# Limited differences of decays on ScalarE's rectifier, and a group's scaling placed beside the last heads, in a two-block decoder kernel

## The chip, the cores and the metric

The kernel runs on one core of a Trainium2 chip. The metric is the device time of one execution in microseconds, the lower the better. Everything is float32 or float32r in memory of the chip; the weights come from HBM.

## What is computed

The input x has 512 positions of 1024 features. The reference is a block of two layers (a state-space mixer and a convolved feed-forward; differential attention and another convolved feed-forward) and a second block (three mixed branches, cross attention, a gated feed-forward). The change touches the state-space mixer alone, whose core is:

```python
def segsum(a):
    cs = jnp.cumsum(a, axis=-1)
    d = cs[..., :, None] - cs[..., None, :]
    return jnp.where(mask, d, -jnp.inf)      # lower triangle

decay_in = jnp.exp(segsum(ac))                                   # per head and chunk, 128 x 128
cb = jnp.einsum('bclgn,bcsgn->bcgls', cc, bc)
y_diag = jnp.einsum('bcgls,bgrcls,bcsgrp->bclgrp', cb, decay_in, xc)
y_off = jnp.einsum('bclgn,bcgrpn,bgrcl->bclgrp', cc, states_in, jnp.exp(a_cs))
...
y = y + xs32 * d_skip.astype(jnp.float32)[:, None]
y = y.reshape(b, s, D_INNER) * jax.nn.silu(z.astype(jnp.float32))
y = rms_norm(y.reshape(b, s, SSM_GROUPS, D_INNER // SSM_GROUPS), ...).reshape(b, s, D_INNER)
return y @ out_w
```

There are 32 heads of 64 features in four groups of eight, and four chunks of 128 positions. Since the decays are sums of negative numbers, a difference cs[l] - cs[s] with l at or behind s is never above 0; in the other triangle it is limited to 0 before the exponential, so that nothing overflows, and the product with the masked cb takes it out.

## The kernel before, in words

**Data.** Activations lie with features on partitions and the 512 positions along the row: one tile of 128x512 for each 128 features. A matrix product is made in float32r from two halves of each operand, a rounded one ("hi", made by ScalarE) and the rest ("lo", made by VectorE), with three matmuls for each 128x128 block of weights. Weights are streamed: SyncE loads units of up to 128x1024 into three buffers, ScalarE rounds them (line 1536 for most), VectorE takes the rest (a cut, line 1972).

**Order of the work.** A planner (class Plan) writes the order down before anything is built. Its time is a tick: one piece of a weight product on TensorE, six matmuls of 128x512, after the small work that is due at that tick. `once(name, key, test, windows)` starts a piece of work at the first tick at which its test holds and PSUM banks are free for its windows. Each engine's program then walks over the ticks, and in a tick over its own list of duties in the order in which they stand in the source; `at("pair", T - 2)` means the duty of every pair that was started two ticks ago. Each engine issues in this order, and waits on semaphores where data comes from another engine (`full` and `empty` of a PSUM bank, and named signals such as `sub`, `edec`, `yadd`).

**State-space stage.** Per group g: six tiles of the convolved inputs (`in`), four gate tiles (`z`), statistics of the chunk states (`sta`, `stb`), then four pairs of heads, three ticks apart, then `gate` (product with the gate tiles, squares, their sums), `rms`, `yn` (scaling by the norm and the splitting in hi and lo as operand Y of the output product), and `out` (eight tiles of the output product, two ticks each). In the plan before, pairs (3,0) to (3,3) start at ticks 179, 182, 185 and 188, the scaling of group 2 at tick 192, gate 3 at 196, rms 3 at 204; `out 1` runs over ticks 181 to 196, `out 2` over 197 to 212, `out 3` from 213. The first group's pairs start at ticks 48, 51, 54 and 57, the second's at 73 to 82, the third's at 123 to 132, the scaling of group 1 at 125.

**A pair (g, p), started at tick t**, with two heads k:

- t, TensorE: two matmuls 64*128 64x512 spread the row of cumulated decays over all partitions, into banks `s0` and `s1`.
- t+1, VectorE (lines 2183 to 2195): for each head and chunk, `ts(d, bank, css, SUB, 0.0, MIN)`: row minus the column of the partition, limited to 0, 128x128 each, eight operations; they wait for the row, and for TensorE's `by` of the pair before the last, which read the same buffer.
- t+2, ScalarE (lines 1673 to 1684): for each head an exponential of the spread row itself (64x384, out of the bank, into `ep`), which waits for the differences of that head and for GpSimd's `yadd` of the pair before the last, and empties the bank; then for each head the exponential of the whole difference tile, 128x512.
- t+3, TensorE: `bo`, the product with the states. GpSimd (line 2546): the two difference tiles times the masked cb (128x512 each).
- t+4, VectorE: `bo` times `ep` (128x384).
- t+5, TensorE: `by`, matmuls 128*64 128x128 for both heads and all chunks.
- t+6, VectorE: the skip term; t+7, GpSimd: the sum (128x384).

Beside this run, on ScalarE, the first tap and the tanh of each convolution, the tanh of each gate tile, the squares of `gate`, the hi halves of Y, and at the end of a tick the rounding of a weight unit. In ScalarE's list a tanh of a convolution comes ahead of the pair's exponentials. VectorE has for each convolution three taps and a product (line 1975), for `yn` four products at ticks T to T+3 and four rests at T+2 to T+5, for `gate` four products in one tick, ahead in the list of `yn` and behind the pair's duties; the cut of a weight unit is last in a tick. Helpers record most operations, so line 1972 is any two-tile operation of VectorE, 1975 any scalar-tensor-tensor, 1980 a tensor-scalar with two operations, 1536 a ScalarE copy, 1539 a ScalarE function, 2546 a two-tile operation of GpSimd, 1142 a matmul.

The condition that places the scaling of groups 2 and 3 is in `free` in the planner (line 409):

```python
return ("z", 3, 3) in self.end and (g == 3 or self.past("pair", (3, 3), 4))
```

Of the kernel before, what the change touches and what calls it, by code (L numbers as in the profile page):

```python
# [13 lines left out]
ACT = mybir.ActivationFunctionType  # L14
MUL, ADD, SUB, MIN, MAX, POW = ALU.mult, ALU.add, ALU.subtract, ALU.min, ALU.max, ALU.pow
AX = mybir.AxisListType.X

P = 128
# [3 lines left out]
NT = S // P  # L22
# [131 lines left out]
class Plan:  # L154
# [22 lines left out]
    def at(self, name, t):  # L177
        return self.starts.get(name, {}).get(t, ())
# [182 lines left out]
    def ssm(self):  # L361
# [24 lines left out]
        def have(keys, more=0):  # L386
            return all(k in silu and self.T >= silu[k] + more for k in keys)

        for g in range(4):
            self.once("sta", g, lambda g=g: have([("in", g, 0), ("in", g, 1)], 4)  # L390
                      and (g == 0 or self.past("pair", (g - 1, 3), 6)), [(("bt", g), 0, 2), (("scb", g), 0, 2)])
            self.once("stb", g, lambda g=g: have([("in", g, i) for i in range(2, 6)], 2) and self.past("sta", g, 2)
                      and self.past("dec", 0, 13),
                      [(("xc", g, c), c, 2) for c in range(NT)] + [(("st", g, c), 5 + 2 * c, 2) for c in range(3)])
            for p in range(4):
                self.once("pair", (g, p), lambda g=g, p=p: self.past("stb", g, 8)
                          and (p == 0 or self.past("pair", (g, p - 1), 3)),
                          [(("s0", g, p), 0, 3), (("s1", g, p), 0, 3), (("bo", g, p), 3, 2), (("by", g, p), 5, 2)])
            self.once("gate", g, lambda g=g: self.past("pair", (g, 3), 8) and have([("z", g, i) for i in range(4)], 1))

            def squares(g=g):
                if self.when("gate", g) == self.T:
                    for i in range(1, 4):
                        self.sq_n[("g", g), i] = len(self.sq_n)
                if self.past("gate", g, 8 if g in (0, 3) else 11) and self.when("rms", ("g", g)) is None:
                    self.rms(("g", g))

            self.rules.append(squares)

            def free(g=g):  # L410
                if g == 0:
                    return self.past("tabs", 0, 48)
                if g == 1:
                    return ("out", 0, 7) in self.end
                return ("z", 3, 3) in self.end and (g == 3 or self.past("pair", (3, 3), 4))

            self.once("yn", g, lambda g=g, free=free: self.past("rms", ("g", g), 6) and free())

            def parts(g=g):
                if self.when("yn", g) == self.T:  # L420
                    for i in range(4):
                        self.lo[f"Y{g}", i] = self.T + 2 + i

            self.rules.append(parts)
# [531 lines left out]
def by_block(ap, n=32):  # L956
    return ap.rearrange("p (j h) -> p j h", h=n)


def again(ap, n):  # L960
    return ap.unsqueeze(1).to_broadcast([P, n, ap.shape[1]])
# [18 lines left out]
class Kernel:  # L980
# [12 lines left out]
    def full(self, key):  # L993
        return self.sig.bank[self.plan.bank[key]].full, self.turn(key)
# [7 lines left out]
    def leave(self, key):  # L1002
        return self.sig.bank[self.plan.bank[key]].empty, 1
# [525 lines left out]
def scalar_program(eng, K):  # L1529
    plan, buf, sig, dram = K.plan, K.buf, K.sig, K.dram  # L1530
    at, full, empty, leave = plan.at, K.full, K.empty, K.leave
    w = Waits(eng)
    pc = buf.pc

    def copy(out, in_, scale=1.0):
        return eng.activation(out, in_, ACT.Copy, scale=scale)  # L1536

    def func(f, out, in_, bias=0.0, scale=1.0, accum=None):
        return eng.activation(out, in_, f, bias=bias, scale=scale, accum_out=accum)  # L1539
# [78 lines left out]
    def ssm(T):  # L1618
        for key in at("conv", T - 1):
            _, g, i = key  # L1620
# [10 lines left out]
        for key in at("conv", T - 3):  # L1631
            _, g, i = key
# [3 lines left out]
        for key in at("zsilu", T - 1):  # L1636
            _, g, i = key
# [30 lines left out]
        for g in at("stb", T - 6):  # L1668
            w.wait_ge(*full(("st", g, 0)))
            if g:  # L1670
                w.wait_ge(*full(("bo", g - 1, 3)))
            copy(buf.St[:, 0, :], K.of(("st", g, 0))[:, :]).then_inc(*leave(("st", g, 0)))
        for g, p in at("pair", T - 2):
            n = 4 * g + p
            e_ = buf.ep[n % 2]
            for k in range(2):
                rows = slice(64 * k, 64 * k + 64)
                w.wait_ge(*sig["sub"].at(g, p, k))
                if n >= 2:
                    w.wait_ge(*sig["yadd"].at((n - 2) // 4, (n - 2) % 4))  # L1680
                func(ACT.Exp, e_[rows, P:S], K.of((f"s{k}", g, p))[rows, P:S]).then_inc(*leave((f"s{k}", g, p)))
            for k in range(2):
                d = buf.hd[2 * (n % 2) + k]
                func(ACT.Exp, d[:, :], d[:, :]).then_inc(*sig["edec"].up(g, p, k))
        for age, ii in ((1, (0, 1)), (2, (2,)), (3, (3,))):
            for g in at("gate", T - age):
                for i in ii:
# [277 lines left out]
def vector_program(eng, K):  # L1965
    plan, buf, sig = K.plan, K.buf, K.sig
    at, full, empty, leave = plan.at, K.full, K.empty, K.leave
    w = Waits(eng)
    pc = buf.pc

    def tt(out, a, b, o):
        return eng.tensor_tensor(out, a, b, o)  # L1972
# [4 lines left out]
    def ts(out, a, s0, o0, s1=None, o1=None):  # L1977
        if o1 is None:
            return eng.tensor_scalar(out, a, s0, None, o0)  # L1979
        return eng.tensor_scalar(out, a, s0, s1, o0, o1)  # L1980
# [138 lines left out]
    def ssm(T):  # L2119
        for _ in at("dec", T - 2):  # L2120
            bank = K.of(("d1",))
# [15 lines left out]
        for _ in at("dec", T - 8):  # L2137
            bank = K.of(("d2",))
# [3 lines left out]
            for j in range(NT):  # L2142
                t = eng.tensor_copy(by_block(buf.csd[:, j, :]), again(buf.css[:, 32 * j:32 * j + 32], 4))
            t.then_inc(*sig["csd"].up())
            tt(buf.tail[:, :], bank[:, P:2 * P], buf.css[:, :], SUB).then_inc(*sig["tail"].up())
        for _ in at("dec", T - 13):
            w.wait_ge(*sig["csh"].at())
            for rows in LOW_ROWS:
                t = tt(buf.csT[rows, :], K.of(("d3",))[rows, :], buf.csT[rows, :].bitcast(F), SUB)
# [27 lines left out]
        for g, p in at("pair", T - 4):  # L2177
# [2 lines left out]
            w.wait_ge(*empty(("s0", g, p)))  # L2180
            w.wait_ge(*empty(("s1", g, p)))
            tt(e_[:, P:S], K.of(("bo", g, p))[:, P:S], e_[:, P:S], MUL).then_inc(*leave(("bo", g, p)))
        for g, p in at("pair", T - 1):
            n = 4 * g + p
            for k in range(2):
                d, bank = buf.hd[2 * (n % 2) + k], K.of((f"s{k}", g, p))
                w.wait_ge(*full((f"s{k}", g, p)))
                w.wait_ge(*sig["cs"].at())
                if n >= 2:
                    w.wait_ge(*full(("by", (n - 2) // 4, (n - 2) % 4)))  # L2190
                for c in range(NT):
                    a = slice(c * P, c * P + P)
                    col = 32 * c + 8 * g + 2 * p + k
                    t = ts(d[:, a], bank[:, a], buf.css[:, col:col + 1], SUB, 0.0, MIN)
                t.then_inc(*sig["sub"].up(g, p, k))
        for g, p in at("pair", T - 6):
            xs = buf.XS[g % 2][:, p, :]
            w.wait_ge(*full(("by", g, p)))
# [17 lines left out]
        for key in at("conv", T - 2):  # L2216
            _, g, i = key
# [6 lines left out]
        for key in at("conv", T - 4):  # L2224
            _, g, i = key
# [3 lines left out]
        for key in at("zsilu", T - 2):  # L2229
            z = buf.ZT[key[1] % 2][:, key[2], :]  # L2230
# [601 lines left out]
```

## Time and profile before

| | |
|---|---|
| median of three runs | 2459.2 us (2458.94 to 2461.61) |
| the profiled execution | 2459.41 us, its span in the trace 2457.6 us |
| mean granted TensorE clock | 0.995 |
| TensorE busy | 2418.4 us, 98% |
| VectorE busy | 1398.4 us, 57% |
| ScalarE busy | 972.2 us, 40% |
| GpSimd busy | 406.3 us, 17% |

The state-space stage fills about the first 430 us of the span. In the profile, times are microseconds from the span's start, PE is TensorE's matrix unit, DVE VectorE, ACT ScalarE and POOL GpSimd. The granted clock is the share of full speed (2.4 GHz) that the throttle gave TensorE. Ends of matmuls are modelled, so an idle time of PE is a little smaller than the distance that it makes in the starts.

### The profile page before, as it was taken

What the parts mean: (1) busy time and instruction counts of PE and PEld (TensorE: products, weight loads), DVE (VectorE), ACT (ScalarE), POOL (GpSimd) and SP (SyncE); (2) the same over time, 40 slices, a digit from 0 to 9 for tenths busy, and PEclk for the clock granted to TensorE, in tenths of its full rate; (3) what the DMA queues carried; (4) which work ended last, traced back from release to release, by engine and by line L of the source; (5) the groups of instructions that cost most, each with busy time, mean ns of one, the idle gap of its engine ahead of it and who ended that gap; (6) DMA issues with size and microseconds to landing.
All of it is one profiled execution on the core that took longest, in us unless ns stands there. A gap on an engine that the chain in (4) does not pass through costs nothing.

```text
span 2457.6 us, 30359 instructions
## 1 busy us (share of the span) xinstructions
PE 2418.4 (98%) x11930; PEld 1963.1 (80%) x11930; DVE 1398.4 (57%) x2286; ACT 972.2 (40%) x1595; POOL 406.3 (17%) x320
## 2 busy tenths in 40 slices
PE   8899999999999999999999999999999999999998
PEld 6677777888888887878888887787788887888887
DVE  6878876663665445576546547534565445343342
ACT  5444434442344444454334434424443334322223
POOL 0352332220111222122002100001220101110011
PEclk9999999999999999999999999999999999999999
DMA  4532222223223221132232242231234322223222
GB/s 160 101 88 86 78 69 77 95 94 102 96 84 122 65 69 51 48 113 97 90 105 91 81 137 78 69 112 53 65 120 134 120 87 85 98 91 102 96 84 87
DMA packets 74269, 226.23 MB, mean 92 GB/s; under 512 B 8080, under 2 KB 12304, under 8 KB 74000
## 3 DMA queue, kind: packets, MB, share of 16 engines
q1 hardware_dynamic: 69696, 215.90, 27.2%
q10 hardware_dynamic: 4432, 8.39, 2.0%
q8 instruction: 95, 1.56, 0.3%
q14 instruction: 46, 0.38, 0.0%
HBM read 215.87 MB, written 8.39 MB: 91 GB/s over the span
## 4 chain that ended last, share of the span: by engine, by line
PE 59%; issue 0%; DVE 0%; ACT 0%; POOL 0%; POOLq 0%; DVEq 0%
PE bank L1142 58%; PE bank L1146 1%; ACT t L1536 0%; DVE t L1972 0%; DVE t L1979 0%; DVE t L1975 0%; ACT t L1539 0%; POOL t L2546 0%; POOLq L2767 0%; DVEq L2767 0%; DVE t L2468 0%; DVE t L2474 0%; POOLq L765 0%
## 5 line engine op out<-in xcount | busy, mean ns | idle before, releaser
L1142 PE MATMUL bank<-t 128*128 128x512 f32 (+4 forms) x11412 | 2388.0, 375 | 29.2 <-DVE t L1972 14.9
L1142 PEld LDWEIGHTS bank<-t 128*128 128x128 f32 (+1 forms) x11412 | 1907.7, 186 | 468.2 <-issue 85.3
L1536 ACT ACTIVATE t<-t 128x1024 fp32r<-128x1024 f32 (+5 forms) x649 | 549.3, 856 | 684.2 <-PE bank L1142 277.3
L1972 DVE TENSOR_TENSOR t<-t 128x1024 fp32r<-128x1024 f32 (+6 forms) x686 | 624.7, 921 | 251.4 <-ACT t L1536 246.4
L2546 POOL TENSOR_TENSOR t<-t 128x512 f32<-128x512 f32 (+5 forms) x240 | 365.7, 1530 | 1650.6 <-ACT t L1539 549.0
L1972 DVE TENSOR_TENSOR t<-bank,t 128x512 f32<-128x512 f32 (+4 forms) x410 | 275.6, 676 | 490.1 <-PE bank L1142 472.3
L1539 ACT ACTIVATE t<-t 128x512 f32<-128x512 f32 (+5 forms) x545 | 330.6, 616 | 536.9 <-DVE t L1972 328.1
L1975 DVE SCALAR_TENSOR_TENSOR t<-t 128x512 f32<-128x512 f32 (+6 forms) x430 | 321.1, 752 | 94.8 <-ACT t L1539 54.0
L1536 ACT ACTIVATE t<-bank 128x512 f32<-128x512 f32 (+4 forms) x150 | 71.5, 493 | 130.5 <-PE bank L1146 90.6
L2549 POOL TENSOR_SCALAR t<-t 128x128 f32<-128x128 f32 (+3 forms) x64 | 40.0, 630 | 389.0 <-ACT t L1536 252.7
L1146 PE MATMUL bank<-t 128*128 128x128 f32 x518 | 81.5, 275 | 2.1 <-ACT t L1536 1.0
L1975 DVE SCALAR_TENSOR_TENSOR t<-t,bank 128x512 f32<-128x512 f32 x64 | 46.1, 721 | 63.2 <-PE bank L1142 49.5
L1146 PEld LDWEIGHTS bank<-t 128*128 128x128 f32 x518 | 62.9, 141 | 18.1 <-DVE t L1983 3.0
L1983 DVE CUSTOM_DVE_ANT_0 t<-bank,t 128x256 f32<-128x256 f32 (+3 forms) x128 | 55.6, 463 | 18.9 <-PE bank L1142 16.3
L1975 DVE SCALAR_TENSOR_TENSOR t<-bank,t 128x512 f32<-128x512 f32 x32 | 22.1, 690 | 60.3 <-PE bank L1142 60.3
L1539 ACT ACTIVATE t<-bank 64x384 f32<-64x384 f32 (+2 forms) x41 | 20.5, 501 | 50.2 <-DVE t L1980 28.6
L1979 DVE TENSOR_SCALAR t<-t 128x256 f32<-128x256 f32 (+6 forms) x88 | 33.7, 384 | 2.9
L1980 DVE TENSOR_SCALAR t<-bank,t 128x128 f32<-128x128 f32 x128 | 34.4, 340 | 0.5 <-PE bank L1142 0.5
L1536 ACT ACTIVATE t<-bank,t 128x256 f32<-128x256 f32 (+2 forms) x40 | 16.9, 482 | 39.1 <-PE bank L1142 37.4
L1980 DVE TENSOR_SCALAR t<-bank 128x4 f32<-128x4 f32 (+2 forms) x37 | 6.0, 161 | 35.1 <-PE bank L1142 35.0
L1539 ACT ACTIVATION_READ_ACCUMULATOR t<-t 128x1 f32 x128 | 24.2, 189 | 0.0
L1539 ACT ACTIVATE t<-bank,t 128x256 f32<-128x256 f32 x16 | 7.6, 474 | 37.7 <-DVE t L2468 37.7
(26 smaller groups left out, 60.1 us busy)
## 6 DMA issues: line engine op xcount, KB each, us to landing
t<-in_w SPq DMA_DIRECT2D x304, 512.0 KB, 3.4
t<-in_w SPq DMA_DIRECT2D x48, 384.0 KB, 3.0
t<-in_w SPq DMA_DIRECT2D x56, 320.0 KB, 2.9
t<-in_w SPq DMA_DIRECT2D x28, 256.0 KB, 3.2
tab<-t ACTq DMA_DIRECT2D x1, 2560.0 KB
t<-in_x SPq DMA_DIRECT2D x8, 256.0 KB, 5.6
t<-tab SPq DMA_DIRECT2D x8, 256.0 KB, 3.8
spill<-t ACTq DMA_DIRECT2D x1, 2048.0 KB, 8.2
```

The lines of the kernel that those rows point to most:

```text
L1142: return eng.matmul(out, lhs, rhs, start=start, stop=stop, skip_group_check=loose)
L1146: return eng.transpose(out, in_, ident[0:n, 0:n])
L1536: return eng.activation(out, in_, ACT.Copy, scale=scale)
L1539: return eng.activation(out, in_, f, bias=bias, scale=scale, accum_out=accum)
L1972: return eng.tensor_tensor(out, a, b, o)
L1975: return eng.scalar_tensor_tensor(out=out, in0=a, scalar=s, in1=b, op0=o0, op1=o1)
L1979: return eng.tensor_scalar(out, a, s0, None, o0)
L1980: return eng.tensor_scalar(out, a, s0, s1, o0, o1)
L1983: return eng.tensor_tensor_reduce(out, a, b, 1.0, FMAX, ADD, MIN, m)
L2546: return eng.tensor_tensor(out, a, b, o)
L2549: return eng.tensor_scalar(out, a, s, s1, o, o1)
```

## The change

The limited differences of a pair leave VectorE's list and stand in ScalarE's, one tick after the pair's start as before. ScalarE computes them with the opposite sign: Relu(-row + column), the column being the bias of each partition and -1.0 the scale. The exponential that follows has the scale -1.0, which turns the sign back. The exponentials of the spread row no longer wait for the differences of their head but for the row alone (they follow the differences in ScalarE's own order), and the exponentials of the difference tiles now have the wait for them. In the planner, the scaling of group 2 waits for pair (3, 2) plus 3 ticks in place of pair (3, 3) plus 4.

```diff
@@ class Plan, ssm, free
-                return ("z", 3, 3) in self.end and (g == 3 or self.past("pair", (3, 3), 4))
+                return ("z", 3, 3) in self.end and (g == 3 or self.past("pair", (3, 2), 3))
@@ scalar_program, ssm
+        for g, p in at("pair", T - 1):
+            n = 4 * g + p
+            for k in range(2):
+                d, bank = buf.hd[2 * (n % 2) + k], K.of((f"s{k}", g, p))
+                w.wait_ge(*full((f"s{k}", g, p)))
+                w.wait_ge(*sig["cs"].at())
+                if n >= 2:
+                    w.wait_ge(*full(("by", (n - 2) // 4, (n - 2) % 4)))
+                for c in range(NT):
+                    a = slice(c * P, c * P + P)
+                    col = 32 * c + 8 * g + 2 * p + k
+                    t = func(ACT.Relu, d[:, a], bank[:, a], buf.css[:, col:col + 1], -1.0)
+                t.then_inc(*sig["sub"].up(g, p, k))
         for g, p in at("pair", T - 2):
             n = 4 * g + p
             e_ = buf.ep[n % 2]
             for k in range(2):
                 rows = slice(64 * k, 64 * k + 64)
-                w.wait_ge(*sig["sub"].at(g, p, k))
+                w.wait_ge(*full((f"s{k}", g, p)))
                 if n >= 2:
                     w.wait_ge(*sig["yadd"].at((n - 2) // 4, (n - 2) % 4))
                 func(ACT.Exp, e_[rows, P:S], K.of((f"s{k}", g, p))[rows, P:S]).then_inc(*leave((f"s{k}", g, p)))
             for k in range(2):
                 d = buf.hd[2 * (n % 2) + k]
-                func(ACT.Exp, d[:, :], d[:, :]).then_inc(*sig["edec"].up(g, p, k))
+                w.wait_ge(*sig["sub"].at(g, p, k))
+                func(ACT.Exp, d[:, :], d[:, :], scale=-1.0).then_inc(*sig["edec"].up(g, p, k))
@@ vector_program, ssm
-        for g, p in at("pair", T - 1):
-            n = 4 * g + p
-            for k in range(2):
-                d, bank = buf.hd[2 * (n % 2) + k], K.of((f"s{k}", g, p))
-                w.wait_ge(*full((f"s{k}", g, p)))
-                w.wait_ge(*sig["cs"].at())
-                if n >= 2:
-                    w.wait_ge(*full(("by", (n - 2) // 4, (n - 2) % 4)))
-                for c in range(NT):
-                    a = slice(c * P, c * P + P)
-                    col = 32 * c + 8 * g + 2 * p + k
-                    t = ts(d[:, a], bank[:, a], buf.css[:, col:col + 1], SUB, 0.0, MIN)
-                t.then_inc(*sig["sub"].up(g, p, k))
```

## Rows read from the trace of the kernel before

**Rows 1.** Page, part 1: busy time, share of the span and instructions of each engine

```profile
PE 2418.4 (98%) x11930; PEld 1963.1 (80%) x11930; DVE 1398.4 (57%) x2286; ACT 972.2 (40%) x1595; POOL 406.3 (17%) x320
```

**Rows 2.** Waits of TensorE, 0 to 460 us: total us, times, longest

```profile
PE bank L1142 <- DVE t L1972: 13.2, 9, 3.0
...
PE bank L1142 <- ACT t L1539: 2.4, 1, 2.4
```

**Rows 3.** TensorE's timeline, 345 to 455 us: start, length, tiles, count, idle time before

```profile
369.94 0.96 PE L1142 MATMUL bank<-t 128*128 128x512 f32 x3 [0.69 <-DVE t L1972]
372.96 1.65 PE L1142 MATMUL bank<-t 128*128 128x512 f32 x3 [2.05 <-DVE t L1972]
375.77 15.93 PE L1142 MATMUL bank<-t 128*128 128x512 f32 x65 [1.16 <-DVE t L1972]
...
401.95 36.21 PE L1142 MATMUL bank<-t 128*128 128x512 f32 x155 [1.97 <-DVE t L1972]
```

**Rows 4.** TensorE's timeline, 103 to 118 us

```profile
104.04 9.35 PE L1142 MATMUL bank<-t 128*64 128x128 f32 x64 [0.85 <-DVE t L1972]
115.80 2.58 PE L1142 MATMUL bank<-t 64*128 64x512 f32 x8 [2.41 <-ACT t L1539]
```

**Rows 5.** TensorE's timeline, 246 to 256 us

```profile
255.23 0.98 PE L1142 MATMUL bank<-t 128*64 128x128 f32 x14 [1.25 <-POOL t L2546]
```

**Rows 6.** TensorE in four stretches: length, busy (matmuls), granted clock, DMA share, GB/s

```profile
368.90:379.60 10.70, 6.79 (x17) 0.68 0.15 49
500.00:550.00 50.00, 50.00 (x223) 1.00 0.27 87
113.20:120.20 7.00, 4.58 (x14) 0.76 0.61 105
249.75:252.20 2.45, 2.45 (x14) 1.00 0.00 0
```

**Rows 7.** VectorE's timeline, 360 to 376 us (a merged row may hold several tile types)

```profile
366.52 1.51 DVE L1972 TENSOR_TENSOR t<-t 128x512 fp32r<-128x512 f32 x1
...
369.21 4.83 DVE L1972 TENSOR_TENSOR t<-t 128x512 fp32r<-128x512 f32 x7
...
374.56 1.16 DVE L1972 TENSOR_TENSOR t<-t 128x512 fp32r<-128x512 f32 x1
```

**Rows 8.** Groups by form, 93 to 375 us: count, busy us, mean ns, idle before

```profile
L1980 DVE TENSOR_SCALAR t<-bank,t 128x128 f32<-128x128 f32 x128 | 34.4, 340 | 0.5 <-PE bank L1142 0.5
...
L1539 ACT ACTIVATE t<-bank 64x384 f32<-64x384 f32 x32 | 15.5, 485 | 37.5 <-DVE t L1980 28.6 <-POOL t L2546 8.7
```

**Rows 9.** Busy time of PE, PEld, DVE, ACT, POOL; then clock, DMA share, GB/s

```profile
94.00:129.00 35.00, 31.66 (x180) 23.52 (x180) 29.44 (x58) 16.45 (x27) 17.74 (x12) 0.95 0.60 109
```

**Rows 10.** Groups of ScalarE by form, 0 to 420 us

```profile
L1539 ACT ACTIVATE t<-bank 128x128 f32<-128x128 f32 x1 | 0.3, 258 | 0.0
```

**Rows 11.** ScalarE's timeline, 405 to 408 us: copy with a column as scale, square without

```profile
405.71 0.72 ACT L1536 ACTIVATE t<-t 128x512 fp32r<-128x512 f32 x1 [2.80 <-DVE t L1972]
406.34 0.62 ACT L1539 ACTIVATE t<-t 128x512 f32<-128x512 f32 x1
```

**Rows 12.** ScalarE's timeline, 102 to 118 us

```profile
108.75 1.06 ACT L1536 ACTIVATE t<-t 128x1024 fp32r<-128x1024 f32 x1
114.61 0.63 ACT L1539 ACTIVATE t<-t 128x512 f32<-128x512 f32 x1 [4.80 <-DVE t L1975]
...
115.27 0.99 ACT L1539 ACTIVATE t<-bank 64x384 f32<-64x384 f32 x2
116.28 1.67 ACT L1539 ACTIVATE t<-t 128x512 f32<-128x512 f32 x3
```

**Rows 13.** VectorE's timeline, 102 to 118 us

```profile
110.20 2.15 DVE L1980 TENSOR_SCALAR t<-bank,t 128x128 f32<-128x128 f32 x8
112.27 2.31 DVE L1975 SCALAR_TENSOR_TENSOR t<-t 128x512 f32<-128x512 f32 x3
```

**Rows 14.** GpSimd's timeline, 244 to 262 us

```profile
249.69 6.34 POOL L2546 TENSOR_TENSOR t<-t 128x512 f32<-128x512 f32 x3 [4.34 <-ACT t L1539]
257.86 4.48 POOL L2546 TENSOR_TENSOR t<-t 128x512 f32<-128x512 f32 x3 [1.82 <-ACT t L1539]
```

## The prediction

> **What bounds the kernel now.** I read the page first: TensorE is busy for 98% of the span [rows 1]. So an edit on another engine is worth only what it takes out of TensorE's stops, and the next view is the list of TensorE's waits over the first 460 us, which hold the state-space stage [rows 2]. It is short: 13.2 us on VectorE's line 1972 in nine stops, and 2.4 us on ScalarE in one. Then each stop is found in TensorE's timeline. Three lie in a row where the third group's output projection begins: 0.69, 2.05 and 1.16 us [rows 3]. One of 2.41 us lies at the fourth pair of the first group, with 0.85 us before it [rows 4]. One of 1.25 us lies in the third group [rows 5].
>
> A stop costs more than its idle time, since the clock falls behind it. Undisturbed, 223 matmuls start in 50 us, one each 0.225 us [rows 6]. Around the three stops 17 start in 10.70 us, at a mean granted clock of 0.68: at full pace they take 17 x 0.225 = 3.8, so this place costs **6.9 us**. Around the 2.41 us stop 14 matmuls take 7.00 us; the same 14 (two row spreads of 64x512, six of 128 columns, six of 512) take 2.45 us in the third group, so this place costs **4.55 us** [rows 6].
>
> **What holds the three stops.** Time in this kernel's program is a tick, one weight piece on TensorE. Walking the planner's rules, pair (3,3) starts at tick 188, group 2's scaling (yn) at 192, gate 3 at 196, and out 2's first matmul is at tick 197. Each engine issues in tick order. VectorE writes the second halves of Y2 at ticks 194 to 197, so the last two stand behind the four gate products of tick 196: one merged row of seven operations, 4.83 us long, from 369.21 [rows 7]. TensorE's starts at 369.94, 372.96 and 375.77 each follow such a write. The last one, 1.16 us from 374.56, ends 0.05 us before the third start.
>
> **The change, part by part.**
> *yn 2 four ticks earlier.* The new rule, pair (3,2) plus 3, is met at tick 188; its other conditions (statistics from 155, z 3 finished at 180) are met long before. The twelve vector operations (four scalings on VectorE, four roundings on ScalarE, four rests on VectorE) keep their number and move to ticks 188 to 193, all ahead of the gate and four ticks ahead of out 2. At 6 x 0.225 = 1.35 us a tick the cover is over 5 us, against 1.5 us for the dearest rest [rows 7]. No DMA moves; the weight cut of tick 192 now stands behind fewer operations. **Term A: -6.9 us** (0 if something else is as late; -6.9 is all there is). The 1.97 us stop at group 3's projection [rows 3] hangs on statistics taken 8 ticks after gate 3, whose tick does not change: 0.
>
> *The limited differences leave VectorE.* 128 operations, 34.4 us in all, 0.269 each, so 2.15 per pair [rows 8]. VectorE is busy 29.44 of 35.00 us around the first group's pairs; ScalarE 16.45 [rows 9].
>
> *They come to ScalarE.* The trace has no Relu. The nearest row is a ScalarE operation on a 128x128 bank tile, 258 ns [rows 10]; one with a column as scale takes 0.72 against 0.62 us without [rows 11], so +0.1 for the pointer. Three operations of 128x512 span 1.67 us [rows 12] where alone each takes 0.62, so neighbours overlap by some 0.1. Hence 0.26 us apart and **2.2 us per pair**, the same as on VectorE. Bounds: 0.16 apart if the pointer is free (1.4 per pair), and 0.62 apart if a short tile costs what 512 columns do (5 us). I take 0.26, the nearest row.
>
> The Trainium skill (ScalarE: Activation LUTs, Rules for kernel authors) speaks against this: relu belongs on VectorE. The row agrees on no such loss, 0.26 against 0.27 us for this fp32 tile out of a bank. The same page (What ACT_TABLE_LOAD costs) gives 186 ns + 0.833 per column + 93 per pointer with 93 overlap, an estimate of 0.29 us apart and 2.35 per pair; the sum would be the same within its bounds.
>
> What covers it: ScalarE now stands idle for 28.6 us in front of its bank exponentials, waiting for just these differences [rows 8]. VectorE starts them late because in its order a product that needs the previous pair's second matmul comes first. On ScalarE they start when the row spread lands. The chain from there is: differences 2.2, two bank exponentials 1.0, the first exponential of a whole tile 0.6, GpSimd's two products. It grows by 0.5 to 1, since the bank exponentials no longer overlap the differences. With 16 pairs and the mean wait of 28.6 / 16 = 1.8 us given back, most pairs gain about 1 us of slack; the first pair of each group, where VectorE was prompt, loses about 1.
>
> *Group 0.* The chain of the 2.41 us stop reads backwards as: row spread of pair (0,3) waits for the bank that the exponential at 115.27 empties; this stands behind a tanh at 114.61, which idled 4.80 us for the taps on VectorE; the taps (112.27, 2.31 us) stand behind eight differences (110.20, 2.15) [rows 12, 13]. By then VectorE has issued 24 of these, 6.4 us. With them gone the taps are done near 110. ScalarE's own queue is next: weight split at 108.75, eight Relus to 112.0, tanh to 112.6, exponential to 113.1, against TensorE ready at 113.2 for the spread. So a remainder of about 0.3: **Term B: -4.2** (0 to -4.55).
>
> *Pair (0,0).* Its 0.85 us stop is on VectorE's bank product; that comes 2 us earlier, but the exponentials follow the eight Relus, and GpSimd's products end near 104 too. **Term C: -0.3** (-0.85 to +0.9).
> *Pair (2,1).* TensorE waits 1.25 us for GpSimd, whose three operations take 6.34 us where the next pair's take 4.48 [rows 5, 14]: group 1's scalings run on VectorE beside them. They start some 0.5 us earlier. **Term D: -0.4** (-1.25 to +1). Term A puts yn 2 beside pair (3,3) in the same way; a like stretch of 2 us there falls into the slack that the earlier exponentials give: 0.
> *Pair (1,0).* Relus behind a tanh and before a split and a square move the first product of GpSimd from 154.3 to about 155.9, so the state matmul may wait: **Term E: +0.5** (0 to +1.6).
>
> Sum: -6.9 - 4.2 - 0.3 - 0.4 + 0.5 = **-11.3**. The profiled execution took 2459.41, 0.2 above the median of 2459.2 shown, so it goes to 2448.1 and the median to about **2448**. Everything behind 450 us is the same program.
>
> **Rivals.** 0.2% is 4.9 us, about what a measurement of this kernel can tell from no change.
> 1. *Forecast*, 2448: chance 0.58.
> 2. *Only A comes.* ScalarE has 27 operations in 35 us around group 0 [rows 9] and gets 32 more with the four pairs, 8.8 us: 25 of 35 us busy, with waits in order (and little room within a pair, rival 4). If the tanh or the split (its weights arrive just at 108.7) holds the Relus, the stop at the fourth pair comes back under ScalarE's name: 2459.2 - 6.9 = 2452. For it: the thin margin in B. Against it: VectorE's 6.4 us. 0.25.
> 3. *Only B comes.* The roundings of Y2 stand behind pair (3,3)'s Relus and exponentials on ScalarE, and out 2 still waits: 2459.2 - 4.4 = 2455, within 0.2%. Against it: four ticks. 0.05.
> 4. *Slower: ScalarE becomes the bound of the pairs.* Place: every pair. A pair comes each 6.2 us at full pace (two ticks 2.7, the 14 matmuls 2.45, the state matmuls 1.0 [rows 5, 6]). ScalarE has 2.1 us of exponentials in it (0.99, and two of the three in 1.67 [rows 12]), the rest of its 16.45 us over some 14 ticks, 1.7 per three, and now 2.2: 6.0. The margin is thin, though only four pairs come in a row and the groups beside output projections hold fewer taps. At the bound of 5 us for eight Relus it loses 2.6 x 16 = 42, and the total is 2459 - 7 + 42, near 2494. It decides against the change from 0.7 us lost per pair, 3.1 us for eight Relus, 0.39 apart. 0.06. A change of ScalarE's function table at each Relu would act alike; the trace shows tanh, exponential and copy beside each other without one. The Trainium skill (ScalarE: Activation LUTs, Table sets: the hidden batching unit) says relu is in every set, which no run here shows yet.
> 5. *Nothing*: both stops are replaced by equals, 2459. 0.06.
>
> **How the numbers follow.** Faster by over 0.2%: rivals 1 and 2 and a little of 3, 0.84; within: 3 and 5, 0.09; slower: 4 and a little of 5, 0.07. Range: all the gains at their ends, 2459.2 - 6.9 - 4.55 - 0.85 - 1.25 = 2445.6, taken as 2445; rival 2 with E and C at their dear ends, 2452.3 + 2.5, 2454.8, taken as 2454.5.
>
> **What would show it.** In the profile after: no stop of TensorE on line 1972 at out 2, and granted clock 1.0 there; the stop at the fourth pair of group 0 gone or under 0.5 us; ScalarE busy 35 us more, VectorE 34 less; 128 ScalarE operations of 128x128 at about 0.35 us, 0.26 apart; no new table load; ScalarE's idle time before the bank exponentials mostly gone. Wrong would be: Relus over 0.39 us apart, a new stop at each state matmul on GpSimd, or lateness of Y2 under ScalarE's name.

## The result, and the profile after

| | before | after |
|---|---|---|
| median (lowest to highest), four runs each | 2459.07 us (2458.46 to 2461.61) | 2444.97 us (2442.07 to 2446.79) |
| ratio to before | | 0.9943, 95% interval 0.993 to 0.9955 |
| the profiled execution, its span | 2459.41, 2457.6 us | 2445.11, 2443.3 us |
| mean granted clock | 0.995 | 0.997 |

The kernel is 14.1 us faster by the medians of four runs each (11 to 17 by the interval), where 11 had been forecast. The first part of the page of the kernel after answers to [rows 1]:

```profile
PE 2412.1 (99%) x11930; PEld 1959.0 (80%) x11930; DVE 1367.6 (56%) x2158; ACT 1004.5 (41%) x1723; POOL 403.0 (16%) x320
```

VectorE has 128 instructions and 30.8 us less, ScalarE 128 and 32.3 us more. TensorE does the same 11930 matmuls in 6.3 us less of busy time: a matmul at half clock counts as busy for twice as long, so what stood behind the stops went with them. The waits of TensorE over 0 to 460 us answer to [rows 2]:

```profile
PE bank L1142 <- DVE t L1986: 8.5, 5, 3.0
...
PE bank L1142 <- ACT t L1539: 0.8, 2, 0.5
```

Line 1986 of the kernel after is line 1972 of before (VectorE's two-tile operations), 1989 is 1975, and 2547 is GpSimd's 2546. VectorE's share fell from 13.2 us in nine stops to 8.5 in five, ScalarE's from one of 2.4 to two with 0.8. Of the five, the two longest, 3.0 us each, are ahead of all the pairs and are in every kernel of this case. TensorE's timeline of the kernel after shows where the rest is, against [rows 3 to 5]:

```profile
86.81 25.09 PE L1142 MATMUL bank<-t 128*128 128x512 f32 x128 [2.98 <-DVE t L1986]
112.43 13.29 PE L1142 MATMUL bank<-t 64*128 64x512 f32 x82 [0.53 <-ACT t L1539]
...
245.53 16.66 PE L1142 MATMUL bank<-t 64*128 64x512 f32 x101 [0.30 <-ACT t L1539]
...
349.62 29.26 PE L1142 MATMUL bank<-t 128*128 128x512 f32 x156
...
389.14 31.13 PE L1142 MATMUL bank<-t 128*128 128x512 f32 x133 [1.97 <-DVE t L1986]
```

The row from 86.81 runs without a stop past 102.55, where the state matmuls of pair (0,0) now start: the 0.85 us is gone. The 2.41 us stop is 0.53. The 1.25 us stop on GpSimd is gone, and 0.30 us stands at the row spread of the pair behind it. The row from 349.62 holds the beginning of out 2 with no stop at all. The stop of 1.97 us at out 3 is there as before, 12.81 us sooner. Around out 2's start (the same columns as [rows 6], then those of [rows 9]) TensorE keeps its clock:

```profile
366.00:377.00 11.00, 11.00 (x54) 9.22 (x53) 5.71 (x9) 2.13 (x2) 4.53 (x3) 1.00 0.44 143
```

54 matmuls in 11.00 us at a clock of 1.00, where 17 stood in 10.70 us at 0.68 [rows 6]. The groups by form of the kernel after, 93 to 375 us, answer to [rows 8]:

```profile
L1539 ACT ACTIVATE t<-bank,t 128x128 f32<-128x128 f32 x128 | 34.7, 382 | 8.4 <-PE bank L1142 8.2
...
L1539 ACT ACTIVATE t<-bank 64x384 f32<-64x384 f32 x32 | 15.6, 487 | 2.4 <-POOL t L2547 2.0
```

A Relu lasts 382 ns by itself, and 34.7 / 128 = 0.27 us passes from one to the next, 2.17 us per pair. The tensor-scalar it replaces lasted 340 ns, with 34.4 / 128 = 0.27 between two [rows 8]. ScalarE's idle time in front of the bank exponentials fell from 37.5 to 2.4 us; 8.4 us now stand in front of the Relus, nearly all of it for TensorE's row spread. No table load was added: three up to 420 us, in both traces.

**Where the 14.3 us of the profiles lie.** The starts of the same matmuls in the two traces:

| start of | before | after | shift | new since the row above |
|---|---|---|---|---|
| row spread of pair (0,0) | 93.32 | 92.90 | -0.42 | start of the program |
| state matmuls (`by`) of (0,0) | 104.04 | 102.55 | -1.49 | -1.07, term C |
| `by` of (0,3) | 127.98 | 123.04 | -4.94 | -3.45, term B |
| `by` of (1,0) | 158.92 | 154.23 | -4.69 | +0.25, term E |
| `by` of (2,3) | 267.94 | 262.34 | -5.60 | -0.91, term D |
| `by` of (3,3) | 361.82 | 356.22 | -5.60 | 0 |
| out 3, behind its stop | 401.95 | 389.14 | -12.81 | -7.21, term A |
| end of the span | 2457.6 | 2443.3 | -14.3 | -1.5, none |

The last row has no cause in the change. Near 970 us in the trace after, and near 980 in that before, in the attention, both traces have the same stop of 1.67 us on VectorE; the clock falls behind it in one trace and not in the other. The windows around it, of the kernel before and then of the kernel after:

```profile
980.00:990.00 10.00, 10.00 (x72) 9.50 (x70) 4.71 (x18) 4.34 (x14) 1.57 (x2) 0.83 0.18 59
```

```profile
965.00:975.00 10.00, 8.33 (x69) 7.68 (x69) 6.84 (x25) 5.39 (x17) 2.16 (x3) 1.00 0.18 59
```

A mean of 0.83 over 10 us is 3.4 us at half speed, 1.7 us lost, about what the last row of the table shows. It does not follow the edits: of the twelve kernels' profiles in this case, the clock falls there in those of before, e7, e9, e10 and e11, and not in the other seven. The first row is not the change's either, since the first pair starts anywhere from 92.14 to 95.02 us in these profiles. So some 12.4 us of these two traces are the change's, and 1.9 are chance of this pair of executions.

### The profile page after: what moved, and what is told of

Same layout as the page of the kernel before. It is cut to its first block, busy times and chain, and to the rows that moved or that the text cites. A ratio compares the mean times of both kernels' runs of the same rounds, so it can differ in the third digit from the quotient of the medians.

```text
span 2443.3 us, 30351 instructions
## 1 busy us (share of the span) xinstructions
PE 2412.1 (99%) x11930; PEld 1959.0 (80%) x11930; DVE 1367.6 (56%) x2158; ACT 1004.5 (41%) x1723; POOL 403.0 (16%) x320
## 4 chain that ended last, share of the span: by engine, by line
PE 59%; issue 0%; DVE 0%; ACT 0%; POOL 0%; POOLq 0%; DVEq 0%
PE bank L1142 58%; PE bank L1146 1%; ACT t L1536 0%; DVE t L1986 0%; DVE t L1993 0%; DVE t L1989 0%; ACT t L1539 0%; POOL t L2547 0%; POOLq L2768 0%; DVEq L2768 0%; DVE t L2469 0%; DVE t L2475 0%; POOLq L765 0%
## 5 line engine op out<-in xcount | busy, mean ns | idle before, releaser
L1539 ACT ACTIVATE t<-bank,t 128x128 f32<-128x128 f32 (+1 forms) x144 | 42.3, 392 | 46.1 <-DVE t L2469 37.7
L1539 ACT ACTIVATE t<-bank 64x384 f32<-64x384 f32 (+2 forms) x41 | 20.6, 503 | 15.2 <-PE bank L1142 12.8
```

## The experiments

Each was timed beside runs of the kernel before on the same chip. The ratio is to those; their medians were 2458.52 (e1 to e4), 2457.76 (e5, e7, e9, e11) and 2458.87 us (e6, e10).

### Each part alone: e1_only_yn and e2_only_relu

e1 is the kernel before with this edit alone:

```diff
-                return ("z", 3, 3) in self.end and (g == 3 or self.past("pair", (3, 3), 4))
+                return ("z", 3, 3) in self.end and (g == 3 or self.past("pair", (3, 2), 3))
```

> Group 2's scaling at tick 188, the limited differences still on VectorE. Theory (the three stops at out 2 come from the order of ticks alone): they go, the stops at the first group's pairs (0.85 and 2.41 us) and the 1.25 us one stay, time about 2459.1 - 7.2 = 2452, within 1.5. Rival (the two parts need each other: with the differences still in its list VectorE does the earlier scalings late, or makes a state matmul of group 3 wait): a new stop of over 1 us between 340 and 370 us, time 2454 to 2459.

Measured: 2452.82 us (2449.52 to 2456.56, 11 runs), ratio 0.9977, interval 0.9968 to 0.9986. TensorE's timeline of e1:

```profile
104.61 9.35 PE L1142 MATMUL bank<-t 128*64 128x128 f32 x64 [0.84 <-DVE t L1972]
116.35 4.19 PE L1142 MATMUL bank<-t 64*128 64x512 f32 x14 [2.40 <-ACT t L1539]
...
362.76 23.03 PE L1142 MATMUL bank<-t 128*64 128x128 f32 x114 [0.32 <-POOL t L2546]
...
396.04 4.18 PE L1142 MATMUL bank<-t 128*128 128x512 f32 x17 [1.97 <-DVE t L1972]
```

The three stops of out 2 are gone and the first group's stand, so this edit acts at that place alone. Its pair (0,0) starts 0.56 us later than in the trace of before; less that, out 3 comes 5.91 + 0.56 = 6.5 us sooner. A new 0.32 us on GpSimd stands at the state matmuls of (3,3): there the scaling's operations run on VectorE beside GpSimd's products. The theory's 2452 came (2452.82), and the rival's stop of over 1 us did not.

e2 is the kernel after with the old rule, `(3, 3), 4`.

> The limited differences on ScalarE, group 2's scaling at tick 192 as before. Theory (each part clears its own stops): the first group's and the 1.25 us stop go as in the changed kernel, 5.6 us up to the last pair; at out 2 the stops at the third and fourth operand stay, since the four gate products still come first, though VectorE reaches them a little earlier: 4 to 7 us lost there, time about 2453. Rival (lateness of VectorE, and not the order, made out 2 wait): the three stops go too, time 2446.

Measured: 2449.24 us (2445.7 to 2451.32, 5 runs), ratio 0.9961, interval 0.9948 to 0.9973. TensorE's timeline of e2:

```profile
365.31 0.98 PE L1142 MATMUL bank<-t 128*128 128x512 f32 x3 [0.98 <-DVE t L1986]
368.12 15.76 PE L1142 MATMUL bank<-t 128*128 128x512 f32 x65 [1.83 <-DVE t L1986]
...
394.13 6.25 PE L1142 MATMUL bank<-t 128*128 128x512 f32 x26 [1.97 <-DVE t L1986]
```

The first group is as in the kernel after, but at out 2 two stops are left of three, 2.81 us of idle time instead of 3.90. VectorE, rid of the differences, is less late there also without the new place of the scaling. So the parts overlap: counted from the first pair's start to out 3, they bring 6.5 and 7.4 us alone (the latter 401.95 - 394.13, less 0.46 of an earlier start), 13.9 together if they were independent, and 12.4 in fact. I had expected about 2453 for e2 and missed by nearly 4 us. The place was as the theory said, two stops left at the third and fourth operand, and out 3 comes 5.0 us later than in the kernel after. But I had not counted the 2.2 us that VectorE's relief gives there, and e2's profile gains another 3.1 us behind out 3, where the clock fell neither at the stop of 1.97 us nor near 970 us. e2 also holds the changed waits of the exponentials; what they are worth without moving the differences was not tried.

### ScalarE's margin: e4_relu_twice

The kernel after, with each Relu done a second time into a tile that nobody reads:

```diff
+                    spare = ...
+                    func(ACT.Relu, spare, bank[:, a], buf.css[:, col:col + 1], -1.0)
                     t = func(ACT.Relu, d[:, a], bank[:, a], buf.css[:, col:col + 1], -1.0)
```

> Each limited difference is computed twice on ScalarE, the first time into a spare tile: 2.2 us more per pair. It measures how much room ScalarE has in a pair. Theory (a pair comes each 6.2 to 6.6 us and ScalarE fills 6.0 of it where convolutions run): groups 0 and 1 lose 1.5 to 2 us per pair, groups 2 and 3 less, in all 12 to 25 us, time 2457 to 2470. Rival (ScalarE's idle time elsewhere absorbs it): under 4 us, time below 2449.

Measured: 2459.48 us (2457.84 to 2461.41, 10 runs), ratio 1.0004, interval 0.9995 to 1.0013, and 14.5 above the kernel after. Groups by form of ScalarE, 93 to 375 us, then TensorE's timeline, of e4:

```profile
L1539 ACT ACTIVATE t<-bank,t 128x128 f32<-128x128 f32 x256 | 67.7, 415 | 6.3 <-PE bank L1142 6.0
...
L1539 ACT ACTIVATE t<-bank 64x384 f32<-64x384 f32 x32 | 16.1, 503 | 0.4
```

```profile
107.70 6.72 PE L1142 MATMUL bank<-t 64*128 64x512 f32 x42 [1.63 <-ACT t L1539]
115.61 14.86 PE L1142 MATMUL bank<-t 64*128 64x512 f32 x82 [1.19 <-ACT t L1539]
```

This is the slower rival made real: once ScalarE has 2.1 us more per pair (67.7 less 34.7, over 16), it is never idle before a bank exponential (0.4 us in all), and TensorE waits for it at the row spreads, whose bank it empties. 33 us of work cost 14.5, so some 18.5 were still free, 1.2 us per pair. The time lies in the theory's range; the loss per pair was smaller than it said, 8.3 us against the kernel after by the end of the second group, 1.0 per pair where 1.5 to 2 had been expected. Since e4 takes what before takes, it is about the break-even itself: 67.7 / 16 = 4.2 us of Relus per pair, where the prediction had put it at 3.1.

### Less on ScalarE: e3_head_each

The kernel after, with head 0 of each pair on ScalarE and head 1 on VectorE as before (its exponential keeps the scale 1.0):

```diff
@@ scalar_program
-            for k in range(2):
+            for k in range(1):
...
                     t = func(ACT.Relu, d[:, a], bank[:, a], buf.css[:, col:col + 1], -1.0)
@@ vector_program
+            for k in range(1, 2):
...
+                    t = ts(d[:, a], bank[:, a], buf.css[:, col:col + 1], SUB, 0.0, MIN)
```

> Head 0 of each pair on ScalarE, head 1 on VectorE, four operations each. Theory (the 0.53 and 0.30 us stops left are ScalarE's queue being full by a little): ScalarE is relieved by 1.1 us per pair, both go, time 2443 to 2445. Rival (VectorE's queue in group 0 was the real bound, with its 1.1 us per pair it is late again): the stop at pair (0,3) grows to 1 us or more and the time is 2446 to 2449.

Measured: 2445.56 us (2442.72 to 2449.23, 5 runs), ratio 0.9947, interval 0.9935 to 0.9959: the kernel after's time. TensorE's timeline of e3, at the fourth pair:

```profile
112.44 7.81 PE L1142 MATMUL bank<-t 64*128 64x512 f32 x47 [0.20 <-ACT t L1539]
```

The 0.30 us of the third group is gone. It stands with 0.30 to 0.31 us in the profiles of after, e2, e6, e9 and e11 and nowhere in e3 or e10, so it did hang on ScalarE's length. (e4, with twice the Relus, has 1.19 us there.) The 0.53 us is 0.20, but that e3 did this is not shown: with all Relus on ScalarE the same stop is 0.52 us in e2, 0.36 in e11 and absent in e6 and e9. There is no more in it than these 0.6 us, too little for the timing, and the expected 2443 to 2445 can't be told from what was measured. The rival's stop of 1 us or more did not come. With half of the differences moved, the kernel is as fast as with all of them.

### Why out 2 stopped: e5_gate3_later, e6_yn_190, e11_yn_191

The prediction held that VectorE's order at out 2, the last rests of Y2 behind gate 3's products, made the stops. e5 is the kernel before, with the gate products of group 3 two ticks later instead of the scaling sooner:

```diff
-        for g in at("gate", T):
+        for g in [*(g for g in at("gate", T) if g != 3), *(g for g in at("gate", T - 2) if g == 3)]:
```

> The kernel before, with the four gate products of group 3 issued by VectorE two ticks later (198 in place of 196), all else in its place. Theory (out 2 waited because these four products stand ahead of the last two rests of Y2 in VectorE's order): the stops of 2.05 and 1.16 us go or shrink to under 0.7 us together, the 0.69 us one stays, and 4 to 6 us are saved at out 2; the statistics of group 3 may come a little late, so time 2453 to 2456. Rival (VectorE is simply full there): the stops stay as long, time 2458.

Measured: 2453.07 us (2450.32 to 2454.95, 10 runs), ratio 0.9979, interval 0.997 to 0.9988. TensorE's timeline of e5:

```profile
368.69 1.67 PE L1142 MATMUL bank<-t 128*128 128x512 f32 x6 [0.69 <-DVE t L1972]
371.62 14.15 PE L1142 MATMUL bank<-t 128*128 128x512 f32 x65 [1.26 <-DVE t L1972]
```

In before, three matmuls stand between the first and the second stop and three between the second and the third [rows 3]. Here six matmuls follow the first, so without moving the scaling the second stop, of 2.05 us, is gone, and the third is there with 1.26 us where it had 1.16. The gate products held the second; the first 0.69 us is not theirs, and the third is not theirs alone. VectorE's timeline of e5, 366 to 375 us, shows what else holds it:

```profile
367.95 2.41 DVE L1972 TENSOR_TENSOR t<-t 128x512 fp32r<-128x512 f32 x3
370.29 0.68 DVE L1972 TENSOR_TENSOR t<-bank,t 128x512 f32<-128x512 f32 x1
370.89 3.08 DVE L1972 TENSOR_TENSOR t<-t 128x512 fp32r<-128x512 f32 x5
```

The first row is two rests of Y2 and the weight cut of tick 196, the second a product out of a bank, and the third begins with the last rest, of tick 197, which TensorE awaits at 371.62; the gate products come behind it. The last rest is thus late by itself: it stands in the tick in which out 2 starts, behind the cut (1.2 us) and the bank product. The time came in the theory's range, 4.7 us saved by the medians, though one of the two stops that it named stayed.

e11 and e6 are the kernel after with the scaling at tick 191 and 190 (188 after, 192 before): `(3, 3), 3` and `(3, 3), 2` in the rule.

> The changed kernel, with group 2's scaling at tick 191 in place of 188, so that only the last rest of Y2 stands behind gate 3's products. Theory (the order against the gate decides, and a relieved VectorE catches up): at most one short stop of 0.2 to 1 us at out 2, time 2445 to 2447. Rival (any distance under four ticks brings the stops back): 3 us or more lost at out 2, time 2448 to 2450.

> The kernel after, with the scaling of group 2 at pair (3, 3) plus 2 ticks, tick 190 (after: 188, before: 192; 191 left one stop of 1.80 us). The last two rests of Y2 then stand at ticks 194 and 195, both ahead of the four gate products of tick 196. Theory (the order against the gate products decides): no stop of TensorE at out 2, and 2444 to 2446 as the kernel after. Rival (the rests must be two ticks or more ahead of their matmuls, VectorE being behind anyway): a stop of 0.5 to 1.5 us on VectorE at the first piece of out 2, and 2446 to 2448.

Measured: e11 2448.97 us (2448.06 to 2450.18, 4 runs), ratio 0.9963, interval 0.9948 to 0.9977; e6 2444.42 us (2442.77 to 2447.16, 5 runs), ratio 0.9947, interval 0.9933 to 0.996. e11's timelines of TensorE and of VectorE, then e6's of TensorE:

```profile
368.15 14.17 PE L1142 MATMUL bank<-t 128*128 128x512 f32 x65 [1.80 <-DVE t L1986]
```

```profile
363.10 7.21 DVE L1986 TENSOR_TENSOR t<-t 128x512 fp32r<-128x512 f32 x7
```

```profile
349.68 28.71 PE L1142 MATMUL bank<-t 128*64 128x128 f32 x153
...
388.64 31.62 PE L1142 MATMUL bank<-t 128*128 128x512 f32 x142 [1.97 <-DVE t L1986]
```

At 191 one rest is still in the gate's tick, behind its four products in a row of 7.21 us, and one stop of 1.80 us is left. I had expected 2445 to 2447 there and a stop of at most 1 us. The time is in the rival's range, 2448 to 2450, but not by the rival's loss of 3 us or more at out 2. The profiles of e11 and of the kernel after differ by 5.1 us: some 2.0 at out 2, 1.4 by a later start of the first pair (94.34 against 92.90), and 1.7 behind out 3, where in e11 the clock fell near 970 us. At 190 both rests are ahead of the gate and there is no stop. So the last rest must stand ahead of the gate products, and, as e5 shows, in a tick before out 2 starts: two of the four ticks of the change were needed.

### Why the fourth pair stopped: e7_exp_first

The kernel before, with the pair's exponentials ahead of the tanh in ScalarE's list: if the 2.41 us came from ScalarE's order, this cures it without relief for VectorE.

```diff
@@ scalar_program: at the head of the list, and taken out behind the taps
+        for g, p in at("pair", T - 2):
+            n = 4 * g + p
+            e_ = buf.ep[n % 2]
...
```

> The kernel before, with the pair's exponentials at the head of ScalarE's list of a tick, ahead of the taps and tanhs. Theory (the 2.41 us stop at pair (0,3) came by ScalarE's order: exponentials behind a tanh that waits for VectorE's taps): the bank exponential follows the differences at 112.3 at once, the stop is under 0.6 us, 3.5 to 4.5 us are saved there, time 2454 to 2455. Rival (VectorE's backlog itself is what made pair (0,3) late): the stop stays over 1.5 us, time 2458.

Measured: 2458.25 us (2455.94 to 2461.26, 10 runs), ratio 1.0003, interval 0.9994 to 1.0013. Timelines of TensorE and of VectorE, of e7:

```profile
106.16 13.40 PE L1142 MATMUL bank<-t 128*64 128x128 f32 x84 [1.26 <-DVE t L1972]
121.12 6.12 PE L1142 MATMUL bank<-t 128*64 128x128 f32 x40 [1.56 <-DVE t L1975]
129.11 2.69 PE L1142 MATMUL bank<-t 128*64 128x128 f32 x22 [1.87 <-POOL t L2546]
```

```profile
112.31 2.15 DVE L1980 TENSOR_SCALAR t<-bank,t 128x128 f32<-128x128 f32 x8
114.37 3.20 DVE L1975 SCALAR_TENSOR_TENSOR t<-t 128x512 f32<-128x512 f32 x3
```

The stop at the spread is gone, as the theory had it, and so is its gain: three come in its place, the first where 0.85 us was. VectorE goes from the differences to the taps with no idle time, some 0.4 us later than before when counted from the first pair's start (95.02 against 93.32). ScalarE's name stood beside the stop, but the debt was VectorE's, and another order on ScalarE only moved the place where it was paid.

### The next stop, and both together: e9_rms_6 and e10_best

e9 is the kernel after with the statistics of group 3 six ticks behind its gate:

```diff
-                if self.past("gate", g, 8 if g in (0, 3) else 11) and self.when("rms", ("g", g)) is None:
+                if self.past("gate", g, 8 if g == 0 else 6 if g == 3 else 11) and self.when("rms", ("g", g)) is None:
```

> The changed kernel, with group 3's statistics taken 6 ticks after its gate in place of 8. In the changed kernel the sums are ready at 369.6 us and TensorE takes them at 372.3, two ticks later. Theory (the 1.97 us stop at out 3 hangs on the tick of the statistics): the stop goes, with the half clock behind it where it comes, 2 to 3.6 us less than the changed kernel, time 2441.5 to 2443. Rival (the sums are then late and TensorE waits for GpSimd at the statistics): a new stop of 1 us or more near 370, time 2444 to 2446.

Measured: **2442.05 us** (2440.83 to 2442.43, 5 runs), ratio 0.9932, interval 0.9918 to 0.9946, the lowest median of this case. The interval overlaps that of the kernel after (0.993 to 0.9955), so the timing does not show the gain over it by itself. Out 3 in TensorE's timeline of e9:

```profile
387.83 32.53 PE L1142 MATMUL bank<-t 128*128 128x512 f32 x146 [0.22 <-DVE t L1986]
```

The 1.97 us are 0.22, as the theory had it. e9's trace also has no stop at the fourth pair, which is not this edit's doing (e6 has none there either). e10 adds e3's division of the heads to it.

> The kernel after, with both edits that helped: head 0's differences on ScalarE and head 1's on VectorE, and the statistics of group 3 taken 6 ticks after its gate. If the leftovers of the first and third group (0.53 and 0.30 us) and the stop at out 3 (1.97 us, and the half clock behind it) are separate places, the gains add: TensorE's stops on ScalarE there 0.2 us or less, out 3's 0.3 us or less, and the time 0.5 us below that of the kernel with the later edit alone (2442.05): 2441 to 2442. Rival: VectorE, which has 64 of the differences again, is late with the scalings of group 3 that now come two ticks sooner; then a stop of 0.5 to 2 us stands at out 3 and the time is 2443 to 2445.

Measured: 2444.12 us (2441.17 to 2446.23, 5 runs), ratio 0.9939, interval 0.9927 to 0.9952: no gain over e9. Timelines of TensorE and of GpSimd (line 2560 here), and a window, of e10:

```profile
369.11 8.22 PE L1142 MATMUL bank<-t 128*128 128x1 f32 x32 [0.97 <-POOL t L2560]
```

```profile
362.87 6.09 POOL L2560 TENSOR_TENSOR t<-t 128x512 f32<-128x512 f32 x3 [1.96 <-ACT t L1539]
```

```profile
372.00:375.00 3.00, 3.00 (x9) 2.29 (x8) 1.78 (x3) 0.00 (x0) 1.93 (x1) 0.56 0.10 19
```

These are the sums of gate 3's squares, which the edit of e9 takes two ticks sooner. They need GpSimd's third square, which ends at 362.87 + 6.09 = 368.96, in e9 at 368.85, so e9 has no room there either: its sums start at 368.99. e10's TensorE arrives 0.9 us sooner (its first pair had started 1.0 us sooner, 92.18 against 93.20), VectorE and GpSimd do not, and it waits 0.97 us; eight matmuls at half clock follow, nine in 3 us. The rival had a late engine, but at out 3, where the stop is 0.22 us as in e9. So the two gains do not add in this execution, for two reasons: e9's trace had no stop at the fourth pair that e3's edit could shorten, and an earlier TensorE meets a stop that had just been hidden.

## Why the prediction was right, point by point

- **Term A, -6.9: right** (-7.2 in the table). The reason given, the last two rests behind the gate products, is shown by e5 for the second stop alone. The third stays in e5 with 1.26 us, because its rest stands in the tick in which out 2 starts, behind a weight cut; e11, where a gate does stand ahead of that rest, has 1.80. The first (0.69 us) was not the gate's: e2 loses it by VectorE's relief, e1 by the earlier scaling. Moving the scaling removes all three causes at once, so the term came out although one of the reasons did not hold.
- **Term B, -4.2: the mechanism right, the size 0.8 high** (-3.4). Its remainder was put at 0.3 us. It is 0.53 us before the first row spread, and the second spread, whose bank the second exponential empties, starts 0.51 us behind the first, where e6 and e9, which have no stop here, start both at once: 1.0 us in all. The clock has no part in it, as the granted clock is 1.00 from 112 to 114 us. ScalarE's timeline of the kernel after, against [rows 12]:

```profile
108.27 1.06 ACT L1536 ACTIVATE t<-t 128x1024 fp32r<-128x1024 f32 x1 [2.54 <-DMA t<-in_w]
109.35 2.17 ACT L1539 ACTIVATE t<-bank,t 128x128 f32<-128x128 f32 x8
111.37 0.68 ACT L1539 ACTIVATE t<-t 128x512 f32<-128x512 f32 x1
...
111.89 1.00 ACT L1539 ACTIVATE t<-bank 64x384 f32<-64x384 f32 x2
```

  The prediction's chain (split, eight Relus, tanh, exponential) is there, 0.5 to 0.7 us sooner, but TensorE was ready for the spread 1.3 us sooner (112.43 - 0.53 = 111.90, against 113.2), having lost the stop at (0,0) and started 0.4 us sooner. It is the weights that seem to set it: ScalarE idled 2.54 us for them. The five profiles with all Relus once on ScalarE agree: the split waits 2.54, 2.53 and 2.35 us in after, e2 and e11, which have the stop, and 0.57 and 0.32 in e6 and e9, which do not. e6:

```profile
106.84 1.06 ACT L1536 ACTIVATE t<-t 128x1024 fp32r<-128x1024 f32 x1 [0.57 <-DMA t<-in_w]
```

- **Term C, -0.3: too small.** The whole 0.85 us went, and with it 0.2 us more (-1.07). The Relus began 0.6 us behind the start of the spread (93.53 and 92.90), where VectorE had begun 2.8 us behind it (96.10 and 93.32); the prediction's "the first pair of each group, where VectorE was prompt, loses about 1" was wrong for the first group.
- **Term D, -0.4: too small** (-0.91). The place was right and the way was not: the products of (2,1) do not start sooner against TensorE but later (3.5 us sooner in the trace, the pair's row spread 4.7). They are shorter: the first took 3.56 us before, while VectorE ran a scaling, a rest and a weight cut (249.62 to 252.09), and takes 1.44 now that VectorE, with no differences in front of these, is past them (the same rest at 244.66 in place of 250.28, the cut done at 246.49). The Trainium skill (GPSIMD Engine Reference, Specifications) says that the two engines share their way to SBUF and contend where VectorE has two inputs there; these rows agree, at 3.56 against 1.44 us; and where GpSimd's next product now meets a rest (247.66), it is the rest that is long, 1.77 us in place of 0.68. GpSimd's row against the first of [rows 14]:

```profile
246.21 4.09 POOL L2547 TENSOR_TENSOR t<-t 128x512 f32<-128x512 f32 x3 [6.46 <-ACT t L1539]
```

- **Term E, +0.5: right in sign** (+0.25).
- **The price of a Relu, 0.26 us apart and 2.2 per pair: right** (0.27 and 2.17). The estimate from the Trainium skill (ScalarE: Activation LUTs, What ACT_TABLE_LOAD costs), 0.29 apart and 2.35 per pair, is 0.02 high; the trace decides. That relu is in every set (Table sets: the hidden batching unit) agrees: no load was added. Its advice that relu belongs on VectorE would have cost this kernel the part of the gain that e2 shows (9.3 us by the medians): the price is the same on both engines, and VectorE was the one in debt.
- **Rival 4** did not come, but it is real: e4 shows it at twice the work. **Rivals 2, 3 and 5** did not come. The thin margin that spoke for rival 2 is real too: what is left of the fourth pair's stop stands under ScalarE's name, behind the weights.
- **The sum**, -11.3, was 1.5 short of the stage's -12.8 (start of the program -0.4, C -0.8, D -0.5, A -0.3, E -0.25, against B +0.8). That it came so close is in part luck: B's shortfall of 0.8 us is offset by what C and D brought beyond their terms. The other 1.5 us to the profile's -14.3 is the clock behind the stop near 970 us, for which the prediction had no term. The median, 2444.97, lies 3 us under the forecast and 0.03 us under the range's low end, which took all the named gains at their ends and left no room for this.

## What to carry to other kernels

An operation that costs the same on two engines belongs on the one that does not set when its readers begin: sum what the late engine owes at the stop (here 24 differences, 6.4 us), not its share of the span. In engines that work in order, the name beside a stop may be only the last in line; follow its own wait back, and move what stands ahead of it there. And after each stop that is removed look for the one that it hid: an earlier arrival is worth nothing where another engine's end is fixed, as GpSimd's square was in e10.

## What was not expected of the hardware

**The same stop does or does not cost the clock.** At out 3 every kernel but e9 and e10 has the same stop of 1.97 us. Windows of 6 us behind it, of before, after, e1, e2 and e6 in turn:

```profile
402.00:408.00 6.00, 6.00 (x19) 4.77 (x20) 3.68 (x5) 2.16 (x3) 0.00 (x0) 0.72 0.38 142
```

```profile
389.00:395.00 6.00, 5.86 (x19) 4.70 (x20) 3.54 (x6) 2.28 (x4) 0.00 (x0) 0.72 0.43 150
```

```profile
396.00:402.00 6.00, 5.96 (x26) 4.92 (x27) 4.46 (x6) 2.35 (x5) 0.00 (x0) 1.00 0.41 145
```

```profile
394.00:400.00 6.00, 5.87 (x26) 4.81 (x27) 4.55 (x7) 2.33 (x4) 0.00 (x0) 1.00 0.42 145
```

```profile
388.60:394.60 6.00, 5.96 (x26) 4.96 (x27) 4.46 (x6) 2.38 (x5) 0.00 (x0) 1.00 0.40 146
```

19 matmuls or 26, so 7 x 0.227 = 1.6 us. Of the ten kernels with this stop the clock falls behind it in before, after, e3, e4, e7 and e11, and not in e1, e2, e5 and e6, which follows none of the edits; what decides it was not found. One profiled execution of each kernel cannot say how often it does. It fits the spread of one kernel's runs, 2442.07 to 2446.79 for the kernel after, though that it makes all of it was not tried. A stop is thus worth its idle time, plus about 1.6 us in some executions: where a forecast takes the clock's share from one profile, it should give both values.
